# A four-layer decoder step: residual kept with features on partitions, its norm by matmul sums inside the next stage

## What is computed

```python
for i in range(DEPTH):                        # DEPTH = 4
    h = mixer[i % 3](x, ...)                  # x @ w_in -> mixing -> @ w_out
    x = layer_norm(DN_ALPHA * x + h, p['ln_g'][i, 0], p['ln_b'][i, 0])
    f = peer(x, p['peer_w_q'][i], ..., p['peer_u'][i], p['peer_v'][i])
    x = layer_norm(DN_ALPHA * x + f, p['ln_g'][i, 1], p['ln_b'][i, 1])

def layer_norm(x, g, b):
    mu = x.mean(-1); var = square(x - mu).mean(-1)
    return (x - mu) * rsqrt(var + 1e-5) * g + b
```

## Time and profile before

| what | us |
|---|---|
| median of 3 runs | 5263.16 |
| lowest and highest | 5262.91, 5264.59 |
| time of the profiled execution | 5264.96 |
| its span, first to last instruction | 5263.2 |
| TensorE busy | 4815.2 (91%) |
| VectorE busy | 3300.9 (63%) |
| ScalarE busy | 2184.5 (42%) |
| GpSimd busy | 661.5 (13%) |
| mean granted TensorE clock, 1.0 is full | 0.932 |

### The profile page before, as it was taken

The page is one execution under the profiler, slowest core; times in us unless marked ns, Lnnn a source line. Parts: engine busy times, 40 slices in busy tenths (PEclk is TensorE's granted clock), DMA queues, the critical chain, the costliest instruction groups (busy, mean ns, idle before and its releaser), DMA issues. The chain is left out here.

```text
span 5263.2 us, 112304 instructions
## 1 busy us (share of the span) xinstructions
PE 4815.2 (91%) x48284; PEld 3633.4 (69%) x48284; DVE 3300.9 (63%) x6417; ACT 2184.5 (42%) x3029; POOL 661.5 (13%) x311
## 2 busy tenths in 40 slices
PE   7799999979588899999975879999998789999997
PEld 3477789975323677799954347778997457778996
DVE  3596778443544776787445259677854359577844
ACT  2475343434101673334433047534343257534343
POOL 0262000000100560000000026300000026200000
PEclk8899999989789999999987579999999789999998
DMA  2444444435153444444440244444443244444443
GB/s 87 129 160 157 149 149 146 159 124 186 46 182 131 147 160 155 149 146 151 160 151 8 62 122 157 160 145 153 145 158 133 78 133 158 157 148 150 145 161 121
DMA packets 289633, 725.93 MB, mean 138 GB/s; under 512 B 26003, under 2 KB 103396, under 8 KB 288116
## 3 DMA queue, kind: packets, MB, share of 16 engines
q1 hardware_dynamic: 289142, 718.74, 40.8%
HBM read 687.98 MB, written 30.67 MB: 137 GB/s over the span
## 5 line engine op out<-in xcount | busy, mean ns | idle before, releaser
L1498 DVE SCALAR_TENSOR_TENSOR b_lo<-raw,b_hi 128x1024 f16<-128x1024 f32 x808 | 989.6, 1225 | 902.4 <-ACT b_hi L1316 897.2
L1400 PE MATMUL ps<-x_hi,b_hi 128*128 128x320 f16 x4608 | 1273.3, 300 | 11.7 <-ACT b_hi L1316 11.4
L1316 ACT ACTIVATE b_hi<-raw 128x1024 f16<-128x1024 f32 x808 | 851.1, 1054 | 1034.5 <-PE ps L1421 1029.1
L1401 PE MATMUL ps<-x_lo,b_hi 128*128 128x320 f16 x4608 | 1273.2, 300 | 0.0
L1418 PE MATMUL ps<-w_hi,b_lo 128*128 128x256 f16 x4096 | 1119.3, 273 | 0.0
L1418 PE MATMUL ps<-w_lo,b_hi 128*128 128x256 f16 x4096 | 1119.1, 273 | 0.0
L1418 PE MATMUL ps<-w_hi,b_hi 128*128 128x256 f16 x4096 | 1118.7, 273 | 0.0
L1421 PE MATMUL ps<-w_hi,b_lo 128*128 128x64 f16 x4096 | 789.4, 193 | 0.0
L1421 PE MATMUL ps<-w_lo,b_hi 128*128 128x64 f16 x4096 | 789.4, 193 | 0.0
L1421 PE MATMUL ps<-w_hi,b_hi 128*128 128x64 f16 x4096 | 789.2, 193 | 0.0
L1404 PE MATMUL ps<-x_hi,b_lo 128*128 128x320 f16 x4608 | 721.4, 300 | 0.0
(11 more groups left out here) (222 smaller groups left out, 7074.3 us busy)
## 6 DMA issues: line engine op xcount, KB each, us to landing
raw<-in_peer_uT SPq DMA_DIRECT2D x512, 512.0 KB, 3.3
raw<-in_peer_v SPq DMA_DIRECT2D x512, 512.0 KB, 3.3
raw<-in_peer_w_q SPq DMA_DIRECT2D x64, 512.0 KB, 5.1
w_in<-in_ret_w_in SPq DMA_DIRECT2D x48, 512.0 KB, 5.3
w_in<-in_sgu_w_in SPq DMA_DIRECT2D x32, 512.0 KB, 7.9
s_in<-in_state_ret SPq DMA_DIRECT2D x32, 512.0 KB, 4.4
out<-s_new SPq DMA_DIRECT2D x32, 512.0 KB, 3.0
w_in<-in_gla_w_in SPq DMA_DIRECT2D x24, 512.0 KB, 7.1
```

The source lines that it names most:

```text
L1316: nc.scalar.activation(b_hi[:, p], raw[:, p], ACT.Copy, scale=scale_of(n)).then_inc(s.hi, 1)
L1400: nc.tensor.matmul(dst, b_hi[:, p, k, :], x_hi[:, k, :], start=(k == 0), stop=False)
L1401: nc.tensor.matmul(dst, b_hi[:, p, k, :], x_lo[:, k, :], start=False, stop=False)
L1498: nc.vector.scalar_tensor_tensor(out=b_lo[:, p].rearrange("p k e -> p (k e)"), in0=raw[:, p].rearrange("p k e -> p (k e)"), scalar=scale_o ...
```

## The change

The residual is now `x_T`, features on partitions (8 x 320 words), and no longer turned. `residual_norm`, the two phases behind PEER and their transposes are gone. In place of them stands `norm`, whose steps are put into the first instructions of `project_in`, of the PEER stage, and of the last phase:

```diff
+        def centre(dve, s):          # VectorE: 4 adds of the residual, then 4 subtractions of the mean
+            for e in range(2):
+                f = slice(4 * e, 4 * e + 4)
+                nc.vector.scalar_tensor_tensor(out=x_T[:, f, 0:PROMPT], in0=x_T[:, f, 0:PROMPT], ... in1=ps[...])
+                nc.vector.scalar_tensor_tensor(out=x_T[:, f, PROMPT:T], ... in1=ps[:, 4, ...]).then_inc(s.n_sum, 1)
+            dve.wait_ge(s.n_mean, 1)
+            for m in range(KT // 2):
+                nc.vector.tensor_tensor(two, two, mean, ALU.subtract).then_inc(s.n_cen, 1)
+        def scaled(dve, s, low=True):
+            dve.wait_ge(s.n_std, 1)
+            nc.vector.reciprocal(sd[:], sd[:]).then_inc(s.n_rs, 1)
+            for k in range(KT + 2):
+                if k < KT: ...       # x_T[k] = x_T[k] * gain[k] * sd
+                if k >= 2 and low: ...   # x_lo[k-2] = x_T[k-2] + shift[k-2] - x_hi[k-2]
+        def squares(act, s): ...     # ScalarE: 4 squares of 640 columns
+        def deviation(act, s): ...   # ScalarE: root of 320 columns, from PSUM
+        def high(act, s, dst=x_hi):  # ScalarE: 8 times x_hi[k] = x_T[k] + shift[k]
+        def sums(pe, s):             # TensorE: 8 float32 matmuls for the mean, 8 for the variance
+            for k in range(KT):
+                last = nc.tensor.matmul(ps[:, 5, 0:T], mean_w[:], x_T[:, k, :], ...)
+            last.then_inc(s.n_mean, 1)
+            for k in range(KT):
+                last = nc.tensor.matmul(ps[:, 6, 0:T], mean_w[:], sq[:, k, :], ...)
+        def offset(pool, s):         # GpSimd: x_T += shift, 2,560 columns, after the last low part
+            pool.wait_ge(s.n_lo, KT)
```

In `project_in` of layers 1 to 3 the low parts of job 0 go from VectorE to GpSimd. Its ScalarE list scales `w_in` in place and then copies, two parts ahead of the root and two behind the high parts of `x`:

```diff
+                    for m in range(PARTS):                       # GpSimd
+                        pool.wait_ge(s.w_hi, m + 1)
+                        nc.gpsimd.tensor_tensor(w_lo[at], w_in[at], w_hi[at], ALU.subtract).then_inc(s.w_lo, 1)
+                    nm.offset(pool, s)
                 if side:
                     side.mask(pool, s)
...
+                            if n == 0 and nm:
+                                pe.wait_ge(s.n_lo, k + 1)        # TensorE, first unit
...
+                    nm.squares(act, s)                           # ScalarE
+                    split(0, range(2))
+                    nm.deviation(act, s)
+                    nm.high(act, s)
+                    split(0, range(2, PARTS))
...
+                    nm.centre(dve, s)                            # VectorE
+                    nm.scaled(dve, s)
+                    dve.wait_ge(s.w_lo, PARTS)
```

`project_out` has its operands exchanged, so that its result has features on partitions, and it loads the first three PEER blocks at its end:

```diff
-                    for i, (t0, r) in enumerate(TILES):
-                        for e, (ss, ww) in enumerate(((s_hi, w_hi), (s_hi, w_lo), (s_lo, w_hi))):
-                            for n in range(2):
-                                last = nc.tensor.matmul(ps[0:r, 2 * i + n, :], ss[:, k, t0:t0 + r], ww[... 512 ...])
+                    for f in range(KT):
+                        for m, (ww, ss) in enumerate(((w_hi, s_hi), (w_hi, s_lo), (w_lo, s_hi))):
+                            lhs = ww[:, k % 4, 128 * f:128 * f + 128]
+                            nc.tensor.matmul(ps[:, f // 2, ...256 columns...], lhs, ss[:, k, 0:PROMPT], ...)
+                            last = nc.tensor.matmul(ps[:, 4, ...64 columns...], lhs, ss[:, k, PROMPT:T], ...)
...
+                for n in range(RING):
+                    sp.dma_start(raw[:, n], query_block(layer, n)).then_inc(s.ahead, 16)
```

In the PEER stage GpSimd makes the low parts of blocks 0 and 1 too (`n < POOL_TO`), ScalarE's list begins with `high(0)`, `high(1)`, squares, `high(2)`, root, high parts of `x`; GpSimd runs `offset` between the low parts of blocks 2 and 3; the write of `x_spill` is issued after the load of block 16 and waits for `offset`:

```diff
+                    if n == 2 * PH:
+                        sp.wait_ge(s.n_x, 1)
+                        sp.dma_start(x_spill, x_T[:]).then_inc(s.spill, 16)
```

More of the change, by code:

```diff
@@ L54 @@
 Side = namedtuple("Side", "signals load mask biases")
+Norm = namedtuple("Norm", "centre scaled squares deviation high sums offset")
+NORM_SIGNALS = ("n_sum", "n_mean", "n_cen", "n_sq", "n_var", "n_std", "n_rs", "n_w", "n_hi", "n_lo", "n_x")
 def ret_log_decay():
@@ L1365, in lists @@
                     nc.scalar.copy(gh_T, gt_T).then_inc(s.gates, 1)
-                for n in range(RING):
-                    high(n)
+                high(0)
+                high(1)
+                nm.squares(act, s)
+                high(2)
+                nm.deviation(act, s)
+                nm.high(act, s)
                 for n in range(total):
@@ L1627, in build, with half_of, _ @@
             peer(layer)
-        with phase("stored") as (block, s):
+        with ExitStack() as ctx, phase(*NORM_SIGNALS, "tp", "out0", "out1", "stored") as (block, s):
+            sq = sb("sq", [128, KT, T], ctx=ctx)
+            sd = sb("sd", [128, T], ctx=ctx)
+            y_tok = sb("y_tok", [128, 3, D], ctx=ctx)
+            nm = norm_of_experts(DEPTH - 1, sq, sd)
+            def half_of(i, e):
+                r = ROWS[i]
+                return y_tok[0:r, i, 512 * e:512 * e + 512], ps[0:r, 2 * i + e, :]
+            @block.vector
+            def _(dve):
+                nm.centre(dve, s)
+                nm.scaled(dve, s, False)
+                for i in range(3):
+                    dve.wait_ge(s.tp, 4 + i)
+                    nc.vector.tensor_copy(*half_of(i, 1)).then_inc(s.out1, 1)
+            @block.scalar
+            def _(act):
+                nm.squares(act, s)
+                nm.deviation(act, s)
+                nm.high(act, s, x_T)
+                for i in range(3):
+                    act.wait_ge(s.tp, 1 + i)
+                    nc.scalar.copy(*half_of(i, 0)).then_inc(s.out0, 1)
+            @block.tensor
+            def _(pe):
+                nm.sums(pe, s)
+                for e in range(2):
+                    pe.wait_ge(s.n_hi, 4 * e + 4)
+                    for i, (t0, r) in enumerate(TILES):
+                        for f in range(4):
+                            last = nc.tensor.transpose(ps[0:r, 2 * i + e, 128 * f:128 * f + 128],
+                                                       x_T[:, 4 * e + f, t0:t0 + r], ident[:])
+                        last.then_inc(s.tp, 1)
```

356 lines of the change are left out of this document (166 added, 190 removed).

## The result

| | before | after |
|---|---|---|
| median, us (4 runs each) | 5263.03 | 5182.79 |
| lowest and highest | 5261.48, 5264.59 | 5181.23, 5184.10 |
| span of the profiled execution | 5263.2 | 5180.8 |
| mean granted clock | 0.932 | 0.946 |

The ratio is 0.9847, with a 95% interval of 0.983 to 0.9864: 1.5% faster. The prediction had 5190 us, in a range of 5155 to 5226. The medians lie 80.2 us apart and the profiled spans 82.4; the sum of the prediction was 72.4.

A forecast was written before the change was run, and what follows sets the result against it. TensorE, busy 91% of the span, was taken as the bound, with the rest mostly at seams. Gains less the copies' cost and clock allowance summed to 72.4 us off 5263.2, so 5190 us was predicted, range 5155 to 5226.

The forecast's parts named there:

- `project_out`, 28.6: In project_out, each tile falls from 4.10 to 3.32 us, first tiles saving less: 28.6 us over 40 tiles.
- Seam A, 4.1 each: Phase start to end of PEER block 1 takes 28.8 us against 32.9: 4.1 us gained at each of four.
- The clock in the sums, 5 us for one or two of eight seams: Norm's float32 sums run at full clock, except one or two seams of eight caught at half: 5 us lost.
- between the two rests after which the clock fell ... I take the full clock: Before the norm's sums, TensorE rests 2.6 us, between 2.45 and 3.5, so full clock was assumed: 4.6 us per eight matmuls.
- rival 1: In all seams, the norm's sums run at half clock, losing 63.7 us in place of 5: 5249 us, chance 0.08.
- rival 3: Half clock lasts until well behind each seam, 28.6 us on top of rival 1: slower, 5278 us, chance 0.03.
- Seam B, 9.6 each: In layers 1 and 2, phase start to end of job 0 takes 44.4 us against 54.0: 9.6 us each.
- Layer 3, 4.5: Layer 3's job 1 weights wait behind GpSimd's offset and memset; its first unit ends at about 53, gaining 4.5 us.
- Last phase, 9.4: Without low parts, the last phase takes 30.1 us against 39.5: 9.4 us gained.
- First phase, -0.7: Six extra copies in the first phase, through ScalarE at 0.6 us each, cost 0.7 us.
- VectorE's low parts of job 1 ... hidden, but by 1.5 us only: Queued behind GpSimd's last part and offset, they finish at 43 us, just before TensorE wants them: 1.5 us to spare.
- The fear of the port: VectorE operations might wait for GpSimd's beside them, 1.1 us per seam A, 4.4 in all; no wait was taken.

The follow-up runs named there:

- pout_only: Kernel before with only project_out's matmul operands exchanged (24 pairs of 256 and 64 columns for 18 of 512): 5230.2 us.
- busy_first: Changed kernel with six float32 matmuls of 128 columns into an unused PSUM bank ahead of each mean sum: 5174.8 us.
- mask_first: Changed kernel with the memset of the mask put ahead of GpSimd's low parts and offset: 5175.7 us.
- busy_all: busy_first with more unused matmuls behind the variance sums and, in project_in's first unit, ahead of part 2: 5173.7 us.
- busy_drip: busy_all with two more unused matmuls ahead of each of the seven later k of PEER block 0: 5166.6 us.

## Why the prediction was right, and where it was off

- **`project_out`, 28.6: right mechanism, 3.8 too small.** A later tile went from 4.11 to 3.32 us, as read from the earlier trace rows; 36 of them give 28.4. The four first tiles gave 3.7 more; the prediction's allowance, half a microsecond each and then 2 us off, was the mis-sized term. (Its terms also give 28.1 rather than the 28.6 taken: 31.2, less 1.1, less 2.) `pout_only` measured the whole at 32.1.
- **Seam A, 4.1 each: 3.7 on average.** Of the chain, the adds (1.6 to the first half), the subtractions and squares, and one sum (4.57 against 4.6) were as worked out. The reciprocal took 2.15 us and not 2.7: the slope from one and eight columns was high, 6.7 ns per column is measured. The estimate from the Trainium skill (VectorE: DVE Perf Modes, § First, the fixed hardware budget), 2.7 as well, does not agree with the trace, and the measurement decides. Against this the mean sums took 1.5 to 1.7 us more. `offset` took 4.46 (5.4 to 5.9 was said) and was hidden, as block 3 followed block 1 by 6.52 us, two full blocks.
- **The clock in the sums, 5 us for one or two of eight seams: wrong in number.** The step "between the two rests after which the clock fell ... I take the full clock" failed: it fell in six of eight mean sums. Its cost at the end of a seam was small, since in the seams A a later root only moves the clock's next fall and rise: taking all six away (`busy_first`) moved block 1 by 0.6 to 0.85 us. The half clock never reached the variance sums, so rival 1 (63.7 us) and rival 3 had their loss in two sums where there was about half of one. The measured rows of the table already hold what the clock cost, so half of the 10 us between the sum of the prediction and the spans is this allowance; the rest is `project_out` (3.8) and layer 3 (4.3), less the seams A and the first phase.
- **Seam B, 9.6 each: 8.4 and 11.0.** The chain was as said: root behind two weight parts and a table load (15.9, predicted 16.4), first unit held by GpSimd's last two low parts. In layer 1 the mean sum at the half clock made the difference. That the two together lie so near 9.6 is luck.
- **Layer 3, 4.5: 8.8.** The wait was foreseen (issue of job 1's weights behind `offset` and memset). Two numbers were off. The issue came at 38.6 and not 41.7, because reciprocal and `offset` were shorter; and before, job 1's first unit ended at 59.1 and not 57.5, because TensorE was at job 0 until 55.8. The step that failed took ScalarE's last part as the end. `mask_first` priced what remained of the wait: 3.8 us.
- **Last phase, 9.4: 9.6.** The last store was issued at t = 25.2, as worked out, but the root came at 14.7 and not 13.6; the shorter reciprocal and transposes (4.7 us for 5.8) made up for it, which is luck.
- **First phase, -0.7: -1.75.** The first transpose starts 0.46 us later, before any copy, which is open. The six copies then alternate with ScalarE's casts in one queue, and the last high part of the input ends at 16.15 us in place of 14.03, the first unit at 31.61 in place of 29.95. The step that failed is "partly under TensorE's waits": of 2.5 us that the copies add to the queue, 1.7 came through.
- **"VectorE's low parts of job 1 ... hidden, but by 1.5 us only": right in layers 1 and 2.** One of them took 5.46 us beside `offset`, and no TensorE wait followed. The fear of the port was right in kind. By the Trainium skill's rule (SBUF — State Buffer, § Who interferes with whom) the adds, subtractions and reciprocal pay nothing. The trace agrees for the adds (0.41 us beside GpSimd and alone) and the reciprocal (2.15); no subtraction ran beside GpSimd in the changed kernel. What the prediction did not see is that the whole order stood on it. It also told the rule without its exception, a VectorE operation in a two-port mode, and one with a single full operand does stand in this trace (last section). The named move to GpSimd was neither gain nor loss as placed (43.4 against 43.1 at job 0), but against the better order, VectorE with `offset` behind it, it costs 4.1 us at job 0 of layer 2 and 5.7 in layer 1, at equal mean sums.

## What to carry to other kernels

When a step is moved to GpSimd, list the VectorE operations that will run beside it and stand for it: those with two operands in SBUF, and those that the trace shows longer beside GpSimd than alone. In these traces the engine that started second stood until the other's operation was through, and a step made earlier on one engine can land in such an overlap and lose all it won. Before an engine's queue is given a long job, look for short steps queued behind it that another queue waits for: one memset behind 13 us of GpSimd work held SyncE and cost 3.8 us. And a seam must be followed to a milestone well behind it: a wait removed ahead of a half-clock stretch moved the stretch and gave back half.

## What the runs showed of the hardware

Reciprocal of 320 columns: 2.15 us on VectorE, with or without GpSimd beside it. A VectorE operation with two SBUF operands stood for GpSimd's whole operation: one low part of 1,024 columns, 1.22 us alone, took 5.46 beside a GpSimd operation of 4.46:

```profile
1173.14 4.46 POOL L280 TENSOR_TENSOR x_T<-x_T,ln_T 128x2560 f32<-128x2560 f32 x1
...
1173.23 5.46 DVE L433 SCALAR_TENSOR_TENSOR w_lo<-w_in,w_hi 128x1024 f16<-128x1024 f32 x1 [5.56 <-POOL w_lo L344]
```

Two SBUF operands are not the only such case. In the mixer of layer 0 a VectorE operation on one full tensor, with a mean and a factor per partition, took 0.81 us alone and 2.87 beside GpSimd's 2.34:

```profile
98.30 0.81 DVE L572 TENSOR_SCALAR v<-v,mv,rs 128x1024 f32<-128x1024 f32 x1
...
100.48 2.87 DVE L572 TENSOR_SCALAR v<-v,mv,rs 128x1024 f32<-128x1024 f32 x1
...
100.46 2.34 POOL L584 TENSOR_TENSOR v<-v,vb 128x1024 f32<-128x1024 f32 x1 [67.33 <-DVE v L574]
```

TensorE's clock fell not only in rests but also while it had work in small pieces (0.54 to 0.60 busy in the rows of `busy_all`), and stayed at 2.4 GHz in all four seams A of `busy_drip`, where the gaps between the pieces were filled with matmuls whose result nobody reads. Over identical code and the same rest of 2.6 us a mean sum was caught by the half clock in layer 1 and not in layers 2 and 3, and layer 1's own took 6.27 us in the changed kernel and 4.57 in `mask_first`. The Trainium skill says of this clock that the same kernel meets it differently from run to run (TensorE: Matmul & The Clock Gate, § What's actually happening); the trace agrees, 4.57 or 6.27 us for the same eight matmuls.
